# Attention in a hybrid diffusion step: maxima from row tiles, folded halves of values, eight tiles of probabilities summed on GpSimd

## The reference

```python
def one_block(qblk):                       # 128 queries
    s = jnp.einsum('bqkgd,bskd->bkgqs', qblk, k).astype(jnp.float32) * scale
    p = jax.nn.softmax(s, axis=-1).astype(v.dtype)
    return jnp.einsum('bkgqs,bskd->bqkgd', p, v)
```

## Time and profile before

| | |
|---|---|
| median of three runs | 3152.87 us (3152.68 to 3153.63) |
| the profiled execution | 3151.15 us, its span 3149.4 us |
| PE busy over the span | 96% |
| DVE / ACT / POOL busy | 61% / 32% / 13% |

### The profile page before, as it was taken

The page is one execution under the profiler, slowest core; times in us unless marked ns, Lnnn a source line. Parts: engine busy times, 40 slices in busy tenths (PEclk is TensorE's granted clock), DMA queues, the critical chain, the costliest instruction groups (busy, mean ns, idle before and its releaser), DMA issues.

```text
span 3149.4 us, 43665 instructions
## 1 busy us (share of the span) xinstructions
PE 3009.5 (96%) x16241; PEld 2511.0 (80%) x16241; DVE 1922.3 (61%) x3490; ACT 995.6 (32%) x1914; POOL 402.7 (13%) x581
## 2 busy tenths in 40 slices
PE   6999989999999999999979998999989999999998
PEld 5888845567998899988978886555778999899997
DVE  4547777755776677766565577676466444544447
ACT  3323344535321112211443233455261221222212
POOL 1012333311000000000020033343010000000002
PEclk9999989999999999999989998999999999999999
DMA  7341210012232223222021112100211110111111
GB/s 293 101 134 37 77 61 0 0 29 78 73 94 68 80 81 108 92 69 92 30 98 56 32 48 82 40 0 27 71 41 54 41 54 28 54 39 43 49 33 74
DMA packets 93847, 201.46 MB, mean 64 GB/s; under 512 B 12433, under 2 KB 13089, under 8 KB 93025
## 3 DMA queue, kind: packets, MB, share of 16 engines
q1 hardware_dynamic: 78240, 151.76, 15.0%
q0 software_dynamic: 15424, 47.25, 4.3%
HBM read 181.88 MB, written 17.08 MB: 63 GB/s over the span
## 4 chain that ended last, share of the span: by engine, by line
PE 62%; issue 25%; DVE 7%; DMA 2%; ACT 2%; DVEq 1%; POOL 1%; POOLq 0%; ACTq 0%; SPq 0%
PE ps L1885 14%; PE ps L1888 14%; PE ps L1889 14%; PE ps L2139 6%; PE ps L2110 3%; PE ps L2129 2%; PE ps L2130 2%; DVE nm L1555 1%; DMA w_raw<-in_w_slots 1%; PE ps L2024 1%; DVE w_lo L511 1%; DMA modw<-in_w_mod 1%; PE ps L1867 1%; PE ps L2099 1%; PE ps L1981 1%
## 5 line engine op out<-in xcount | busy, mean ns | idle before, releaser
L1885 PE MATMUL ps<-hi,w_hi 128*128 128x384 f32 x1584 | 534.7, 338 | 10.7 <-DVE lo L1190 4.9
L1889 PE MATMUL ps<-hi,w_lo 128*128 128x384 f32 x1584 | 532.9, 336 | 0.0
L1888 PE MATMUL ps<-lo,w_hi 128*128 128x384 f32 x1584 | 532.9, 336 | 0.0
L506 ACT CAST w_hi<-w_raw 128x512 fp32r<-128x512 f32 x368 | 215.6, 619 | 751.8 <-PE ps L1885 684.9
L1885 PE MATMUL ps<-w_hi,hi 128*128 128x512 f32 (+1 forms) x1008 | 390.3, 387 | 10.3 <-DVE lo L1190 4.4
L1888 PE MATMUL ps<-w_lo,hi 128*128 128x512 f32 (+1 forms) x1008 | 381.8, 379 | 0.0
L1889 PE MATMUL ps<-w_hi,lo 128*128 128x512 f32 (+1 forms) x1008 | 381.7, 379 | 0.0
L1714 DVE TENSOR_TENSOR ps<-ps,gate 128x512 f32<-128x512 f32 x288 | 201.0, 698 | 241.1 <-PE ps L1889 240.9
L1885 PE MATMUL ps<-w_hi,f_hi 128*128 128x512 f32 x864 | 336.6, 390 | 0.0
L1889 PE MATMUL ps<-w_hi,f_lo 128*128 128x512 f32 x864 | 336.5, 389 | 0.0
L1888 PE MATMUL ps<-w_lo,f_hi 128*128 128x512 f32 x864 | 336.4, 389 | 0.0
(11 more groups left out here) (311 smaller groups left out, 4776.6 us busy)
## 6 DMA issues: line engine op xcount, KB each, us to landing
w_raw<-in_w_slots SPq DMA_DIRECT2D x368, 256.0 KB, 3.2
w_raw<-in_m_slots SPq DMA_DIRECT2D x160, 256.0 KB, 2.9
out<-xr POOLq DMA_DIRECT2D x18, 512.0 KB, 3.2
modw<-in_w_mod SPq DMA_DIRECT2D x4, 2048.0 KB, 15.2
acc<-in_x_in SPq DMA_DIRECT2D x3, 1536.0 KB, 17.2
zq_dram<-stg POOLq DMA_DIRECT2D x18, 256.0 KB, 2.4
xr<-in_x_in POOLq DMA_DIRECT2D x2, 2304.0 KB, 9.3
xr<-out POOLq DMA_DIRECT2D x2, 2304.0 KB, 9.8
```

What stands on the lines that cost most here:

```text
L506: act.copy(w_hi[:, j, :], w_raw[:, j % RAW, :]).then_inc(S["w_hi_done"], 1)
L1885: mm = pe.matmul(out, a_hi, b_hi, start=first, stop=False)
L1888: pe.matmul(out, a_hi, b_lo, start=False, stop=False)
L1889: return pe.matmul(out, a_lo, b_hi, start=False, stop=last)
```

## The change

1. **Maxima on row tiles.** `kst` is laid out so that for the odd sample tiles the high part lies in partitions 64 to 127 and the low part in 0 to 63 (`key_rows`). `scores` no longer multiplies all 128 rows: it takes the high part alone, 64 rows, for the four even tiles (512 columns, bank 0), 64 other rows for the four odd tiles (512 columns, bank 1), and 64 rows for tile 8 (128 columns, bank 2). ScalarE now writes the high part of each key tile twice (into `kst2` and `kst`) instead of copying it over later.
2. **Folded halves.** The two halves of the values are added by a matmul with `fold`, two identities of 64 on top of each other, instead of a transpose and an addition on VectorE. `outputs` on VectorE is one reduction, one reciprocal and one multiplication. The sums are transposed from 64 partitions.
3. **Eight tiles of probabilities on GpSimd.** `psm` = `pr[0]` + ... + `pr[7]` takes seven additions (`SUMS`). `row_sums` is gone; `ninth` waits for the seventh addition and makes both the sums and the values of tile 8. ScalarE's `exp_` waits, before it overwrites `pr[j]`, for the previous step's addition `j`. `PASSES` falls from 6 to 5.
4. **Later sets of maxima.** `SCORES_AT` puts head 1 at `j` = 2, head 2 at `j` = 4 and head 3 at `j` = 6; `ninth` stands at `j` = 2, `outputs_T` at `j` = 4; ScalarE copies values and sums behind its third exponential. `PREP` puts part 2 of the queries behind the second maximum.

```diff
-SCORES_AT = {1: 1, 3: 2, 6: 3}
-PREP = ((0, 1), (), (2,), ())
+SCORES_AT = {2: 1, 4: 2, 6: 3}
+PREP = ((0, 1), (2,), (), ())
-PASSES = 6
-FREED = (1, 1, 2, 2, 6, 6, 6, 5, 5)
+PASSES = 5
+FREED = (1, 1, 2, 2, 3, 3, 4, 4, 5)
+SUMS = NT - 2
...
+        def key_rows(n):
+            return slice(HD, P) if n % 2 and n < NT else slice(0, HD)
...
                     for h in range(HG):
-                        if nk > 1 and h < 3:
+                        if nk > 1:
                             added(h + 1)
                         if nn:
                             diagonal(G, g, h)
+                    for k in range(HG + 1, SUMS + 1) if nk > 1 else ():
+                        added(k)
...
-                    for v in range(HKV):
-                        act.copy(kst2[0:HD, v], kst[0:HD, v])
...
-                    act.copy(kst[0:HD, :, n * P:(n + 1) * P], ps[0:HD, n % 4, 0:2 * P].rearrange("p (a b) -> p a b", b=P)).then_inc(S["k_hi"], 1)
+                    for dst in (kst2[0:HD], kst[key_rows(n)]):
+                        ins = act.copy(dst[:, :, n * P:(n + 1) * P], ps[0:HD, n % 4, 0:2 * P].rearrange("p (a b) -> p a b", b=P))
+                    ins.then_inc(S["k_hi"], 1)
...
-                    if j == 0:
+                    if pk == NT and j < NT - 1:
+                        act.wait_ge(S["sum_done"], START + A - SUMS + max(j, 1))
+                    elif j == 0:
                         act.wait_ge(S["sum_done"], START + A)
...
-                        if pk > 1 and j == min(1, nk - 1):
+                        if pk > 1 and j == min(2, nk - 1):
                             values_out(G - 1, B)
                             sums_out(G - 1, B)
...
-                    dve.tensor_copy(o3, o4[:, :, HD:P])
-                    dve.drain()
-                    dve.tensor_tensor(o3, o3, o4[:, :, 0:HD], ALU.add)
-                    dve.drain()
-                    dve.tensor_tensor(o3, o3, b2(rinv[:, 0], HD), ALU.mult).then_inc(S["oy_done"], 1)
+                    dve.tensor_tensor(o3, o4, b2(rinv[:, 0], HD), ALU.mult).then_inc(S["oy_done"], 1)
...
-                    for b in range(3 if nk == NT else 1):
-                        mm = pe.matmul(ps[:, bank + b, 0:w_], q_hi[:, g, h], kst[:, g, k0 + b * w_:k0 + (b + 1) * w_], start=True, stop=True)
+                    for b in range(2):
+                        a = key_rows(b)
+                        pe.matmul(ps[:, bank + b, :], q_hi[a, g, h], tiles[a, :, b], start=True, stop=True)
+                    a = key_rows(NS)
+                    pe.matmul(ps[:, bank + 2, 0:P], q_hi[a, g, h], kst[a, g, NS * P:NT * P], start=True, stop=True).then_inc(S["s_ps"], 1)
...
+                    pe.wait_ge(S["sum_done"], START + A + SUMS)
                     side(0, 32, 6, ones[:, 0:32], psm[:, g], True, True)
-                    side(32, 32, 6, ones[:, 0:32], pr[:, 4], True, True)
-                    side(64, 32, 6, ones[:, 0:32], pr[:, 5], False, True)
-                    side(96, 32, 6, ones[:, 0:32], pr[:, 6], False, True).then_inc(S["pv_done"], 1)
+                    side(32, 32, 6, ones[:, 0:32], pr[:, 8], True, True)
+                    side(64, 32, 5, vst[:, g, 8, 0:32], pr[:, 8], False, True)
+                    side(96, 32, 5, vst[:, g, 8, 32:HD], pr[:, 8], False, True).then_inc(S["pv_done"], 1)
...
+                        pe.matmul(ps[:, 7, h * HD:(h + 1) * HD], o_s[:, h * P:(h + 1) * P], fold[:], start=True, stop=True)
...
-                        mm = pe.transpose(ps[:, 6, h * P:(h + 1) * P], sm_s[:, h * P:(h + 1) * P], ident[:])
+                        mm = pe.transpose(ps[:, 6, h * P:h * P + HD], sm_s[0:HD, h * P:(h + 1) * P], ident[0:HD, 0:HD])
...
                             pairs(G - 1, e1, 1 - g, 3)
-                            ninth(G - 1, e1, 1 - g)
-                            row_sums(a1, 1 - g)
-                        if pk > 1 and j == min(3, nk - 1):
+                        if pk > 1 and j == min(2, nk - 1):
+                            ninth(G - 1, e1, a1, 1 - g)
+                        if pk > 1 and j == min(4, nk - 1):
```

More of the change, by code:

```diff
@@ L306, in build @@
         qn = put("qn", [HQ * HD])
+        fold = put("fold", [HD])
         put = region(a_m, a_end)
@@ L975, in values_in @@
                 def values_in():
+                    for r in (slice(0, HD), slice(HD, P)):
+                        act.copy(fold[r], ident[r, r])
                     act.wait_ge(S["at_ld"], 48 * L + 48)
-                    act.drain()
-                    for v in range(HKV):
-                        act.copy(kst2[0:HD, v], kst[0:HD, v])
                     for v in range(HKV):
@@ L2192, in step @@
                     G, E, B, A = counts(L, t, g)
[L2193 removed]
+                    e1, a1 = E - pk, A - (SUMS if pk > 1 else 0)
                     for j in range(nk):
```

47 lines of the change are left out of this document (22 added, 25 removed).

## The result

| kernel | median, us | lowest to highest | ratio to before, 95% interval |
|---|---|---|---|
| before | 3153.25 | 3152.68 to 3154.09 | |
| after | 3234.47 | 3230.62 to 3236.24 | 1.0254, 1.0242 to 1.0267 |

The change makes the kernel 81 us slower. The prediction said slower, 3197, and at most 3213: the direction is right, the size is not. The profiled execution of after took 3235.47, with a span of 3233.7 against 3149.4 before, and the 84.3 between the spans can be followed row by row.

A forecast was written before the change was run, and what follows sets the result against it. PE's stream was taken to set the pace, with a DVE chain almost as long that blocks by POOL would lengthen: 28 x 1.5 + 2 = +44 on 3151.15 gives 3195.2, median 1.7 above, 3197; range 3164 to 3213.

The forecast's parts named there:

- Mutual exclusion of DVE and POOL: Attention steps: second and third additions hold DVE's preparation, delaying head 3's scores by 1.76 us; two blocks, chance 0.52.
- The clock: Attention steps: clock must stay at 2.4 GHz; a fall from PE's idle tenth got no chance of its own.
- TensorE's own sum: PE per step: row_sums -0.87, scores -0.94, fold +0.4, shape changes +1.6, waits -0.28; sum -0.1, between -0.6 and +0.8.
- The fold: PE per step: four float32 products in place of four transposes, +0.4 us.
- a change of array shape: PE per step: eight more changes at 0.2 us each, +1.6; by the cheaper entry into 64 columns, 0.14, +1.1.
- `outputs` on DVE, 0.9 shorter, is worth 0: Each step: it lies behind the fourth maximum, ahead of which nobody waits, so its saving is worth 0.
- 28 steps: Both layers' attention: each step goes from 14.49 to 16.0 us, +1.5, counted 28 times.
- Outside the 28 steps: Extra key copies +1 per layer, first step -1, last full step +1; together +2, between -3 and +13.
- The seven additions in front of a `ninth`: Last full step: additions stand ahead of a ninth that comes early; +1, up to 3 x 1.28.
- The first step: First attention step, at 1.2 GHz: shorter scores that its maxima wait for, -1 us.
- Faster: Rival: no blocks, shape changes free, DVE's chain sets a step of 14.0, -0.45; 3140 us, chance 0.08.
- One block: Rival: L1514 gets in ahead of the diagonal, one block per step, +0.65 a step; 3173 us, chance 0.24.

The follow-up runs named there:

- prep_and_pool_moved: After with part 2 of the queries' preparation behind the fourth maximum and GpSimd's second and third additions behind diagonals 0 and 1; 3150.24 us, ratio 0.9989.
- order_alone: Before with only the change's order (later maxima, ninth, outputs_T, part 2); 128-row scores, three additions, no fold; 3203.21 us, ratio 1.0154.
- gaps_filled: After plus unused 512-column products on TensorE, three before head 2's scores and four before head 3's; 3210.09 us, ratio 1.0170.
- row_tiles_alone: Before with only the keys in alternate halves and the 64-row scores and maximum of after; 3147.75 us, ratio 0.9981.
- no_fold: prep_and_pool_moved with the last full step's diagonals first, and the value halves added on DVE after transposes instead of by fold; 3183.26 us, ratio 1.0096.
- three_in_last_step: prep_and_pool_moved with three additions, and the other rows by TensorE, in the last full step of each layer only; 3145.63 us, ratio 0.9975.
- prep_left_out: After with the queries' preparation in the steps replaced by a one-column copy per head group, so outputs are not real; 3145.66 us, ratio 0.9978.
- pool_order_alone: After with only GpSimd's list reordered (additions 2 and 3 behind diagonals 0 and 1), part 2 still behind the second maximum; 3178.61 us, ratio 1.0080.
- full_rows: After with scores on all 128 rows (1152 columns) instead of 64-row tiles; 3207.99 us, ratio 1.0173.

## Why the prediction was right and wrong

- **Mutual exclusion of DVE and POOL, and where it strikes: right.** L1515 1.55 long, L1526 0.67, the copy 1.22; the step at full clock 15.95 against 16.0. The experiments that bear the mechanism out best are `prep_and_pool_moved`, which removes the two blocks with the same instructions in another order, and `order_alone`, which adds them to the kernel before.
- **The clock: the step that failed.** "PE's idle share of about a tenth is the only thing that speaks for a fall, and I give it no chance of its own." The idle share came out as forecast, and with it came falls to 1.2 GHz for +28.8 us. That alone is more than the 21.5 us by which the median lies above the range; the other term too small is the work outside the 28 steps, below. `gaps_filled` shows it: the same steps, no idle time, no fall. Every step before had PE busy at 2.4 GHz without a pause, so the rows that I had read said nothing of what idle time does to the clock, and an effect without a row was set to zero instead of being bounded. But the same trace, outside the attention, has such rows, and I had not read them. Windows of the kernel before, around two falls (the columns as above):

```profile
310.04:313.45 3.41, 1.42 (x12) 1.23 (x11) 3.07 (x5) 2.96 (x6) 0.00 (x0) 1.00 0.71 231
313.45:316.87 3.42, 3.38 (x8) 2.70 (x9) 3.04 (x13) 2.35 (x8) 0.88 (x1) 0.50 0.79 265
1699.27:1702.68 3.41, 3.41 (x44) 3.35 (x43) 0.15 (x1) 0.35 (x1) 0.00 (x0) 1.00 0.00 0
1702.68:1706.09 3.41, 3.41 (x9) 2.68 (x9) 3.25 (x6) 0.00 (x0) 0.00 (x0) 0.50 0.00 0
```

The first comes at the end of a single wait of 2.04 us, which ScalarE ends at 313.49. The second follows no wait at all: PE is busy throughout, mostly with products of 36x36 (L1966). So the trace of before had a fall at one wait of 2 us, and one where small products took the place of a wait; whether small or partly filled products count for less inside an attention step stays open, as above. The Trainium skill describes such falls in "TensorE: Matmul & The Clock Gate", section "HAM oscillation — how this bites in real kernels", for waits of 3 to 5 us on a DMA; here they follow waits of 0.80 and 1.04, with TensorE busy for nine tenths of the step, so the waits that this section describes are longer than those that sufficed here, and the rows decide.
- **TensorE's own sum: the size of a term.** -0.1 forecast; 13.95 - 14.49 = -0.54 measured once the blocks were gone, at the far end of the bounds given (-0.6). The fold costs 0.25, not 0.4, and a change of array shape less than the 0.2 taken, if the other terms of the sum are kept: by `row_tiles_alone`, -0.94 for the scores and five more changes give -0.37, so 0.11 each; by -0.54 with the 0.25, eight changes give (-0.54 + 0.87 + 0.94 + 0.28 - 0.25) / 8 = 0.16 each. These are estimates, since no run measured the -0.94 by itself. The dearer price was from the rows of a matmul behind a change in the earlier trace rows; the cheaper bound (0.14), from the entry into 64 columns, was the better one. That a change of the array's mode costs something is what "TensorEngine Tiling (Array Packing)", section "Key Properties", of the Trainium skill says; 0.11 to 0.16 us is its price here by that estimate. It did not matter to the time, because the chain of DVE lay above it.
- **"`outputs` on DVE, 0.9 shorter, is worth 0": not a property of the fold.** In after itself it was not tested. In another order it is worth over a microsecond (`no_fold`).
- **28 steps: two too many.** Only 26 have a preparation that can be held, and the last of each layer is 0.5 shorter than before: 26 x (15.95 - 14.49) - 2 x 0.5 = 37, near the measured 36.2. With the forecast 16.0 the slip of two steps was 4 us, in the direction of too much.
- **Outside the 28 steps: +2 forecast, at most +13; 7.5 + 4.8 + 7.1 = +19.4 measured.** The seven additions in front of a `ninth` with no step beside it were named with a bound of 3.84; they cost some 2 us of each layer's last intervals by `three_in_last_step`, the fall in them included, and the last intervals as a whole 3.7 to 3.8. The first step, for which I expected a gain of 1 over both layers, lost 4.8. In the first layer the clock stayed at 0.50 over the whole of it (before, 0.61 on the average) and it took 21.06; in the second the clock was 0.62, as before, and it still took 19.56, with PE standing 1.40 us before head 2. Where nothing is held it takes 16.28 at a clock of 0.61 (`prep_left_out`, second layer) and 16.26 at 0.63 (`prep_and_pool_moved`, first layer), 1.6 less than before. So the gain was real, the blocks and waits in this step took 3.3 us from it, and the lower clock 1.5 more in the first layer.
- **The rivals.** "Faster" gave 14.0 a step without blocks, and `prep_left_out` and `prep_and_pool_moved` take 13.95. The agreement is chance: that rival had changes of shape free and DVE's chain setting the step, and in these kernels TensorE sets it (busy 195.41 of 195.95 us) and the changes are not free. What is right in it is the condition, no block, which the change's order does not give. "One block", 15.2, is near `pool_order_alone` (14.8 to 14.95).

## What to carry to other kernels

Before an order is changed, write down for every DVE instruction that reads SBUF which GpSimd instruction will run beside it; putting the long GpSimd ones beside reads of PSUM, and part 2 of the preparation away from them, took 2 us off a 16 us step. On TensorE, idle time in a stream that ran without a pause is not priced by its length: check whether the clock held, and where a wait can't be removed, try work for nothing in it before work is cut. Read in the trace at hand every place where the clock falls, also outside the phase that changes. And let a term with no row of its own stand in the range with a bound.

## What the runs showed of the hardware that was not expected

- TensorE idle for 0.80 and 1.04 us in a step of 15.95 was followed, in 13 of 28 steps, by 3.4 or 6.8 us at 1.2 GHz; the same two waits in the step before it, at 522.25, were not. Falls came on a recurring pattern of steps, not in each.
- Products with no use, filled into these waits, took 24 us off the kernel; on 64 rows of the array they did so as well as on 128.
- `pool_order_alone`, with one wait of 0.79 or 0.93 a step and TensorE idle for 5% of the steps, showed a fall; `order_alone` (1.17, 8% idle) and `full_rows` (9% idle), both with scores on 128 rows, showed none. So neither the length of a single wait nor the share of idle time orders these runs.
- The clock fell for 3.4 us, in the kernel before, behind a stretch in which the profile has TensorE busy throughout, with products of 36x36 (1702.68).
- A GpSimd addition of 1.27 us takes 1.5 beside DVE's splitting of weights (7.98 for five, the gaps between them included): the exclusion works against GpSimd just as against DVE.
